# One adaLN-modulated transformer stack on one core: the first norm's modulation applied on transposed columns

## The reference, cut to what matters

```python
def rmsnorm(x, g):
    y = xf * lax.rsqrt(jnp.mean(xf * xf, axis=-1, keepdims=True) + EPS)
    return (y * g.astype(jnp.float32)).astype(x.dtype)

ada = (c @ w_ada + b_ada)[:, None, :]          # w_ada is (1024, 6144)
shift1, scale1, gate1, shift2, scale2, gate2 = jnp.split(ada, 6, axis=-1)
h = rmsnorm(x, g_norm1) * (1.0 + scale1) + shift1
proj = h @ w_in                                # q, k, v, gates, indexer: 12 parts
# fox attention (forget gates), indexer attention with a bias table,
# branches, w_out; rmsnorm + modulated MLP with squared relu; final rmsnorm
# then second_block: 2 layers, each swiglu FFN / mixer / swiglu FFN with layer norms
```

## Time and profile before

| | |
|---|---|
| median of three runs | 1501.1 us (1496.76 to 1505.11) |
| profiled execution | 1496.24 us |
| its span (first to last instruction) | 1494.5 us |
| mean granted TensorE clock | 0.977 |
| TensorE matmul busy | 1399.2 us, 94% |
| VectorE / ScalarE busy | 828.6 us, 55% / 644.4 us, 43% |
| GpSimd busy | 71.3 us, 5% |
| DMA | 268.87 MB, mean 180 GB/s |
| chain of waits, by engine | TensorE 80%, VectorE 8%, DMA 5%, ScalarE 3%, issue 3%, GpSimd 1% |

### The profile page before, as it was taken

How to read it: one execution, slowest core, us unless ns; L and a number is a source line. 1 busy time by engine, 2 the same in 40 slices (tenths; PEclk the granted TensorE clock), 3 DMA queues, 4 the chain that set the end, 5 groups by cost and what they waited for, 6 DMA issues and landing times.

```text
span 1494.5 us, 16234 instructions
## 1 busy us (share of the span) xinstructions
PE 1399.2 (94%) x6296; PEld 1123.1 (75%) x6296; DVE 828.6 (55%) x1117; ACT 644.4 (43%) x1029; POOL 71.3 (5%) x109
## 2 busy tenths in 40 slices
PE   2799999989999999999898999999999999899997
PEld 0577776768888778887776788887788877788886
DVE  6686642676665565455534665446555464755444
ACT  0454442534444354444455454334443344444332
POOL 3100000010000100000100100001000010100000
PEclk9999986999999999999999999999999999999999
DMA  8646753336645466454641565555755544575552
GB/s 309 213 166 199 230 160 100 142 115 223 254 171 198 129 213 207 181 182 157 215 151 59 175 193 206 185 162 167 243 175 181 185 151 160 194 226 172 187 179 84
DMA packets 156478, 268.87 MB, mean 180 GB/s; under 512 B 9543, under 2 KB 101735, under 8 KB 155250
## 3 DMA queue, kind: packets, MB, share of 16 engines
q1 hardware_dynamic: 148578, 239.43, 46.9%
q0 software_dynamic: 7824, 28.41, 5.9%
HBM read 266.74 MB, written 1.07 MB: 179 GB/s over the span
## 4 chain that ended last, share of the span: by engine, by line
PE 80%; DVE 8%; DMA 5%; ACT 3%; issue 3%; POOL 1%; SPq 0%; DVEq 0%; ACTq 0%; POOLq 0%
PE UP L579 15%; PE UP L581 15%; PE UP L580 15%; PE Y L579 8%; PE Y L580 8%; PE Y L581 8%; PE TB L631 3%; DVE WL L1234 3%; PE Y L657 1%; DMA RAW<-in_ffn_w_gu 1%; DMA RAW<-in_a_w_in 1%; ACT WH L948 1%; DMA X<-in_x 1%; DVE Z L1570 1%; PE Y L660 1%
## 5 line engine op out<-in xcount | busy, mean ns | idle before, releaser
L1234 DVE TENSOR_TENSOR WL<-RAW,WH 128x1024 fp32r<-128x1024 f32 (+2 forms) x448 | 510.2, 1193 | 234.2 <-ACT WH L948 231.1
L948 ACT CAST WH<-RAW 128x1024 fp32r<-128x1024 f32 (+2 forms) x448 | 430.4, 1031 | 263.3 <-PE Y L581 155.3
L579 PE MATMUL UP<-WH,AH 128*128 128x512 f32 (+1 forms) x1104 | 447.8, 406 | 22.8 <-issue 11.5
L581 PE MATMUL UP<-WH,AL 128*128 128x512 f32 (+1 forms) x1104 | 435.0, 394 | 0.0
L580 PE MATMUL UP<-WL,AH 128*128 128x512 f32 (+1 forms) x1104 | 434.3, 393 | 0.0
L579 PEld LDWEIGHTS UP<-WH,AH 128*128 128x128 f32 x1104 | 211.1, 191 | 68.0 <-issue 23.3
L581 PEld LDWEIGHTS UP<-WH,AL 128*128 128x128 f32 x1104 | 210.4, 191 | 45.0
L580 PEld LDWEIGHTS UP<-WL,AH 128*128 128x128 f32 x1104 | 211.5, 192 | 40.7 <-issue 0.7
L579 PE MATMUL Y<-WH,HH 128*128 128x512 f32 (+1 forms) x496 | 193.2, 390 | 0.0
L581 PE MATMUL Y<-WH,HL 128*128 128x512 f32 (+1 forms) x496 | 191.5, 386 | 0.0
L580 PE MATMUL Y<-WL,HH 128*128 128x512 f32 (+1 forms) x496 | 191.4, 386 | 0.0
(11 more groups left out here) (191 smaller groups left out, 965.9 us busy)
## 6 DMA issues: line engine op xcount, KB each, us to landing
RAW<-in_ffn_w_gu SPq DMA_DIRECT2D x176, 512.0 KB, 5.1
RAW<-in_ffn_w_down SPq DMA_DIRECT2D x80, 512.0 KB, 4.2
RAW<-in_w_mlp SPq DMA_DIRECT2D x64, 512.0 KB, 4.2
RAW<-in_w_in SPq DMA_DIRECT2D x40, 512.0 KB, 5.2
PIECE<-in_w_ada POOLq DMA_DIRECT2D x32, 512.0 KB, 4.2
RAW<-in_a_w_in SPq DMA_DIRECT2D x24, 512.0 KB, 4.7
WADA<-in_w_ada SPq DMA_DIRECT2D x8, 1024.0 KB, 10.5
RAW<-in_w_out SPq DMA_DIRECT2D x8, 512.0 KB, 3.9
```

The source lines that it names most:

```text
L579: pe.matmul(dst, ah, wh, start=first, stop=False)
L581: return pe.matmul(dst, al, wh, start=False, stop=last)
L948: act.copy(WH[:, u % 2, q * n:(q + 1) * n], RAW[:, q // 2, (q % 2) * n:(q % 2 + 1) * n]).then_inc(wh_done, 1)
L1234: ve.tensor_tensor(WL[:, u % 2, o], RAW[:, q // 2, (q % 2) * n:(q % 2 + 1) * n], WH[:, u % 2, o].bitcast(F32), ALU.subtract).then_inc(wl_d ...
```

## The change

The first norm's modulation is no longer applied on rows (tokens on partitions) but after the transposes, where a channel is a partition, so that scale and shift are one number per partition.

- c, b_ada's first 2048 and g_norm1 are loaded as 32 rows of 128 numbers, and one transpose makes them columns (COLS). The broadcast of g_norm1 and the one-partition load of b_ada go. w_ada's slab k now holds the rows k*128+p.
- ScalarE computes both tiles' sums of squares and x * rstd, copies the table row, and copies the transposed tiles to XT (laid over PIECE).
- VectorE runs the eight slabs in a row, the eighth in two halves of columns, each its own DMA.
- TensorE transposes both tiles, then for each half sums ADA with products of one moving column: ADA's 128x128 blocks are stationary, ONES[:, 0:1] moves.
- VectorE forms SCALE and SHIFT (128x4 per half) and MOD = XT * SCALE + SHIFT (laid over ROWS), ScalarE forms the rounded AH by the same operation, VectorE subtracts to AL. Each of the eight contraction blocks covers both tiles. This alternates with unit 0's weight quarters, and TensorE waits per block (mod_low).
- GpSimd reads the table back only behind the first two pieces; IDENT is built before its DMAs.

```diff
-            sp.dma_start(CC[:, :], t["c"][0].rearrange("(p k) -> p k", k=KT)).then_inc(in_c, 16)
-            sp.dma_start(PIECE[0:1, :, :], t["b_ada"][0:2 * D].rearrange("(o a n) -> o a n", o=1, a=2)
-                         ).then_inc(in_brow, 16)
-            wada = t["w_ada"].rearrange("(p k) n -> p k n", k=KT)
+            sp.dma_start(ROWCOL[24:32, :], t["c"][0].rearrange("(r p) -> r p", p=P)).then_inc(in_c, 16)
+            sp.dma_start(ROWCOL[0:16, :], t["b_ada"][0:2 * D].rearrange("(r p) -> r p", p=P)).then_inc(in_c, 16)
+            sp.dma_start(ROWCOL[16:24, :], t["g_norm1"].rearrange("(r p) -> r p", p=P)).then_inc(in_c, 16)
+            wada = t["w_ada"].rearrange("(k p) n -> p k n", p=P)
...
-            gp.dma_start(ROWS[:, 0, :], t["g_norm1"].partition_broadcast(P)).then_inc(in_rows, 16)
...
-            gp.wait_ge(tmp_v, TMP_V[("h", 1, 1)])
+            gp.wait_ge(ada_done, 2)
+            gp.wait_ge(mod_low, KT)
             step(gp.memset(ADA[:, :, :], 0.0))
...
-            pieces(0, PIECES + 2)
+            pieces(0, 2)
+            table_read(0)
+            pieces(2, PIECES + 2)
...
+            for tok in range(TOK):
+                pe.wait_ge(xhat_done, tok + 1)
+                chain_turns("h", tok, Z)
+            for h in range(2):
+                pe.wait_ge(*((acc_half, 1), (wada_used, KT))[h])
+                for a in range(2):
+                    for k in range(4 * h, 4 * h + 4):
+                        mm = pe.matmul(Y[0][h][:, 4 * a + k % 4:4 * a + k % 4 + 1], ADA[:, a, k * P:(k + 1) * P],
+                                       ONES[:, 0:1], start=True, stop=True)
+                mm.then_inc(ada_done, 1)
...
+            act.wait_ge(in_x, 16)
+            for tok in range(TOK):
+                for h in range(2):
+                    ins = act.activation(Z[:, tok, h * HALF:(h + 1) * HALF], X[:, tok, h * HALF:(h + 1) * HALF], ACT.Square,
+                                         scale=D ** -0.5, accum_out=SQ[:, tok, h:h + 1])
+                ins.then_inc(sq_done, 1)
+            taken(("tab", 0), REVROW[:, :], REV)
+            for tok in range(TOK):
+                act.wait_ge(rs_done, tok + 1)
+                act.activation(Z[:, tok, :], X[:, tok, :], ACT.Copy, scale=RS[:, tok:tok + 1]
+                               ).then_inc(xhat_done, 1)
+            for tok in range(TOK):
+                for h in range(2):
+                    taken(("h", tok, h), XT[:, 4 * h:4 * h + 4, tok * P:(tok + 1) * P], HALF)
+            def mod_highs(h):
+                act.wait_ge(scale_done, h + 1)
+                for k in range(4 * h, 4 * h + 4):
+                    act.activation(AH[:, k, :], XT[:, k, :], ACT.Identity, bias=SHIFT[:, k:k + 1],
+                                   scale=SCALE[:, k:k + 1]).then_inc(mod_high, 1)
             round_unit(0, (0, 1))
-            chain_high("h", 0)
+            mod_highs(0)
             round_unit(0, (2, 3))
+            mod_highs(1)
...
+            for h in range(2):
                 s = slice(h * HALF, (h + 1) * HALF)
+                k = KT - 1
+                ve.wait_ge(*((in_wada[k % 4], 32), (in_last, 16))[h])
+                ve.scalar_tensor_tensor(ADA[:, 0:2, s], WADA[:, k % 4, :].rearrange("p (a n) -> p a n", a=2)[:, :, s],
+                                        CC[:, k:k + 1], ADA[:, 0:2, s], ALU.mult, ALU.add
+                                        ).then_inc((acc_half, wada_used)[h], 1)
+            def modulated(h):
+                q = slice(4 * h, 4 * h + 4)
+                ve.wait_ge(ada_done, h + 1)
+                step(ve.tensor_tensor(SCALE[:, q], Y[0][h][:, 4:8], COLS[:, 8 + 4 * h:12 + 4 * h], ALU.add))
+                ve.tensor_tensor(SHIFT[:, q], Y[0][h][:, 0:4], COLS[:, q], ALU.add)
+                ve.tensor_tensor(SCALE[:, q], SCALE[:, q], COLS[:, 16 + 4 * h:20 + 4 * h], ALU.mult
+                                 ).then_inc(scale_done, 1)
+                ve.wait_ge(scale_done, h + 1)
+                for k in range(4 * h, 4 * h + 4):
+                    ve.tensor_scalar(MOD[:, k, :], XT[:, k, :], SCALE[:, k:k + 1], SHIFT[:, k:k + 1],
+                                     ALU.mult, ALU.add).then_inc(mod_done, 1)
+            def mod_lows(first, end):
+                for k in range(first, end):
+                    ve.wait_ge(mod_done, k + 1)
+                    ve.wait_ge(mod_high, k + 1)
+                    ve.tensor_tensor(AL[:, k, :], MOD[:, k, :], AH[:, k, :].bitcast(F32), ALU.subtract
+                                     ).then_inc(mod_low, 1)
+            split_unit(0, (0,))
+            for h in (1, 3):
+                ve.wait_ge(*emptied(TURN[("h", 1, h // 2)]))
+            modulated(0)
+            mod_lows(0, 2)
+            split_unit(0, (1,))
+            mod_lows(2, 4)
+            split_unit(0, (2,))
+            modulated(1)
+            mod_lows(4, 6)
+            split_unit(0, (3,))
+            mod_lows(6, 8)
```

More of the change, by code:

```diff
@@ L176 @@
 TMP_S = counts(lambda k: k[0] in BY_SCALAR)
-TMP_V = counts(lambda k: k[0] not in BY_SCALAR and k[0] not in ("tab", "flip", "ada", "F", "pool", "y", "my"))
+TMP_V = counts(lambda k: k[0] not in BY_SCALAR and k[0] not in ("col", "h", "tab", "flip", "ada", "F", "pool", "y", "my"))
 TG_NO = counts(lambda k: k[0] in ("up", "gu"))
@@ L476, in step @@
                 gp.wait_ge(g_seq, seq[0])
+            step(gp.memset(IDENT[:, :], 0.0))
+            step(gp.affine_select(out=IDENT[:, :], in_=IDENT[:, :], compare_op=ALU.not_equal, fill=1.0, base=0,
+                                  pattern=[[-1, P]], channel_multiplier=1))
             gp.dma_start(BF[:, :], t["b_forget"].partition_broadcast(P)).then_inc(in_small, 16)
@@ L484, in _ @@
             step(gp.memset(ONES[:, :], 1.0))
-            step(gp.memset(IDENT[:, :], 0.0))
-            step(gp.affine_select(out=IDENT[:, :], in_=IDENT[:, :], compare_op=ALU.not_equal, fill=1.0, base=0,
-                                  pattern=[[-1, P]], channel_multiplier=1))
             step(gp.affine_select(out=TRI[:, :], in_=ONES[:, :], compare_op=ALU.is_ge, fill=0.0, base=0,
@@ L593, in wide @@
                 for k in range(kts):
+                    if u == 0 and tok == 0:
+                        pe.wait_ge(mod_low, k + 1)
                     if chain and k % 4 == 0:
@@ L693, in slot @@
                     values(a - 1)
+            pe.wait_ge(g_seq, 2)
+            pe.wait_ge(in_c, 48)
+            pe.transpose(bank_of(("col",))[:, 0:32], ROWCOL[:, :], IDENT[0:32, 0:32]).then_inc(tr_done, 1)
             pe.wait_ge(in_small, 48)
@@ L717, in _ @@
             rev_row(0)
[L719 to L724, removed]
-            for row, h in parts:
-                pe.matmul(Y[row][h][:, :], ONES[:, :], ADA[:, row, h * HALF:(h + 1) * HALF],
-                          start=False, stop=True).then_inc(ada_done, 1)
-            chain_turns("h", 0, Z)
+            for tok in range(TOK):
[8 more added lines that the diff above has]
+                mm.then_inc(ada_done, 1)
             att = 0
@@ L1347, in _ @@
             ve.tensor_copy(IDR[:, :], IDENT[:, :]).then_inc(cmr_done, 1)
-            ve.wait_ge(in_c, 16)
+            ve.wait_ge(tr_done, TURN[("col",)] + 1)
+            ve.tensor_copy(COLS[:, :], TB[TURN[("col",)] % 2][:, 0:32]).then_inc(tr_free[TURN[("col",)] % 2], 1)
+            ve.wait_ge(*emptied(TURN[("col",)]))
+            step(ve.tensor_scalar(COLS[:, 8:16], COLS[:, 8:16], 1.0, None, ALU.add))
             acc = ADA[:, 0:2, :].rearrange("p a n -> p (a n)")
-            for k in range(KT):
+            for k in range(KT - 1):
                 ve.wait_ge(in_wada[k % 4], 16 * (k // 4 + 1))
@@ L1368, in _ @@
-            ve.wait_ge(in_rows, 16)
-            def modulated(tok, h):
-                s = slice(h * HALF, (h + 1) * HALF)
-                if tok == 0:
-                    ve.wait_ge(ada_done, 2 * h + 2)
-                    step(ve.scalar_tensor_tensor(ADA[:, 1, s], Y[1][h][:, :], 1.0, ROWS[:, 0, s], ALU.add, ALU.mult))
-                step(ve.tensor_tensor(Z[:, tok, s], Z[:, tok, s], ADA[:, 1, s], ALU.mult))
-                ve.tensor_tensor(Z[:, tok, s], Z[:, tok, s], Y[0][h][:, :], ALU.add).then_inc(tmp_v, 1)
@@ L1379, in _ @@
-            modulated(0, 0)
-            modulated(0, 1)
-            chain_low("h", 0)
-            split_unit(0)
-            modulated(1, 0)
-            modulated(1, 1)
-            chain_low("h", 1)
+            for h in range(2):
+                s = slice(h * HALF, (h + 1) * HALF)
+                k = KT - 1
[3 more added lines that the diff above has]
+                                        ).then_inc((acc_half, wada_used)[h], 1)
```

79 lines of the change are left out of this document (37 added, 42 removed).

## The result

The kernel after took 1490.18 us (median of eight runs, 1486.92 to 1495.57), the kernel before 1500.24 us in eight runs on the same chip (1496.53 to 1505.11). The ratio is 0.9933, with the interval [0.9912, 0.9954]: 6.9 to 13.2 us faster. The forecast was 1492 us in 1482 to 1500. The profiled execution took 1487.73 us with a span of 1484.6, at a mean granted clock of 0.977, as before; its span is 9.9 us shorter.

A forecast was written before the change was run, and what follows sets the result against it. The prediction took a chain of waits in the first 62 us as the bound; shorter slabs, modulation and splits let unit 1 start at 53.1 instead of 62.07, 9.0 us gained: median 1501.1 becomes 1492, range 1482 to 1500.

The forecast's parts named there:

- The bound: First 62 us: a chain of waits bounds the start; what is gained at 62.07 should arrive at the end.
- rival (c): Attention slots, 160 to 233 us: TensorE's clock shifts; three more slow periods lose 9.6 us; chance 0.07 slow, 0.08 lucky.
- The sum for the modulation: VectorE's w_ada slabs: with work moved to ScalarE they end at 31.9 instead of 35.5, 3.6 us gained.
- From the sum to the first matmul: One-column products and modulation ahead of unit 0: first matmul at 35.8 instead of 46.72, 10.9 us gained.
- Unit 0's split: VectorE's splits of unit 0's weights: the last WL ends at 41.4 instead of 48.86, 7.5 us gained.
- Unit 1's weights: DMA of unit 1's second half: 5.2 us from issue, landed 47.2 instead of 56.2, 9.0 us gained.
- Rival (b): Weight loads: unit 1's takes 6.91 us again, or table and pieces push unit 2's; gain 5.5, 1495.5 us; chance 0.13.
- Statistics: ScalarE's sums and GpSimd's roots: second root ready 27.6, copies done 31.2, before the products' end at 33.7.
- rival (a): GpSimd's roots come late behind VectorE's slab products, second at 30 to 32.4; gain 6.7, 1494 us; chance 0.12.
- hidden by 2.5 us: ScalarE's copies of the transposed tiles: done at 31.2, covered by the first half's products, which end at 33.7.
- At nothing: Costs taken as zero: the columns' transpose, copy and +1, table-row steps on ScalarE, the later table read.
- The number: Whole kernel: a median of 1492 us, against 1501.1 for the kernel before.

The follow-up runs named there:

- e5: The kernel after with the table's 1 MB read put back ahead of the modulation; 1490.69 us, ratio 0.9920.
- e8: The kernel after with the 512 KB broadcast of g_norm1 loaded again on GpSimd's queue; 1496.27 us, ratio 0.9970.
- e7: The kernel before with only the statistics, the scaled copy and the table row moved to ScalarE; 1496.49 us, ratio 0.9976.
- e1: The kernel after with all of unit 0 rounded and split before the modulation; 1485.40 us, ratio 0.9894.
- e10: The kernel after with 52 extra fp32 matmuls on constants ahead of TensorE's transposes; 1500.19 us, ratio 0.9999.
- e3: The kernel after with x loaded ahead of the first four slabs; 1490.15 us, ratio 0.9921.
- e4: The kernel after with the first half's eight one-column products issued twice; 1495.12 us, ratio 0.9971.
- e2: The kernel after with three small GpSimd loads and the table row moved behind the first half's sums; 1489.47 us, ratio 0.9919.

## Why the prediction was right, point by point

- **The bound.** Right in the main. What the change is shown to gain, it gains ahead of unit 1. "What is gained at 62.07 should arrive at the end" was too smooth: 1.6 us were lost up to the second norm, most of them by the clock at unit 1's start, and 3.6 came on top some 650 us later. The forecast named the attention slots of 170 to 240 us as the place where the clock may turn. Between the two kernels' profiles the number of long periods there didn't change (one of 12.95 us, at 200.80 to 213.75, and before one of 12.98, at 196.84 to 209.82, each with one of 11.4 behind it). But rival (c) is real: five of the variants' profiles have a further period of 13 us and are some 5 us longer there (e5). Whether the slower executions of the kernel after have it (clock down to 0.969) isn't shown.
- **The sum for the modulation**: 3.6 us gained by the slabs' end, 4.1 measured (31.45). e8 confirms the 1.3 us of the broadcast, with 1.4. The row order, the columns' loads and the 2 KB pieces cost little: e8 has them and e7 has not, both have the broadcast, and the slabs end 0.4 us apart (32.85 and 32.48).
- **From the sum to the first matmul**: the half's 16 instructions were priced at 3.0 us and took 3.29; the choice in the middle of 1.8 and 5.3 held. The four multiply-adds at 0.25 each took 1.15 on the path (0.29 each), the small steps 0.16. The first matmul came at 37.16 and not 35.8. That step failed: the second half's 16 instructions stand ahead of unit 0 in TensorE's order, and I had let unit 0 start between. It cost nothing, as unit 0 isn't on the path (e1).
- **Unit 0's split**: forecast 41.4, measured 41.92.
- **Unit 1's weights**: the term that was off most. I took 5.2 us from issue to landing, it was 6.02; with an issue 0.36 us later (42.36 for 42.0) the half lands 1.2 us late (48.38 for 47.2), and unit 1 starts 1.1 us late (54.24 for 53.1). The reason given, that half 0 just ahead in the queue had made it 6.91, isn't borne out either: in e1 the halves are issued 1.9 us apart and the load takes 5.77 us, in the kernel after they are 4.6 us apart and it takes 6.02, in e10, as far apart, 4.44. What sets this time is open. Rival (b) was half right: of its 1.7 us (6.91 for 5.2), 0.8 came.
- **Statistics**: the second root ends at 26.88, forecast 27.6, so rival (a) did not occur. Yet the "hidden by 2.5 us" was wrong, and this is the step of the mechanism that failed. The sum set the end of ScalarE's copies against the end of the products. But TensorE's order puts all transposes ahead of the products, and the second tile's transposes (28.67 in the chain) wait for ScalarE's first copy of the first tile, which ScalarE's order puts behind the second tile's scaled copy (to 28.05). From the root to the last transpose it took 3.7 us, to 30.6, where the first half's sum is there at 30.2. The cover was nothing, and it was luck that this cost no more than some tenths (e3). GpSimd's rows:

```profile
20.58 0.30 POOL L533 TENSOR_SCALAR VAR<-SQ 128x1 f32<-128x1 f32 x1 [14.38 <-ACT Z L1060]
20.96 0.57 POOL L534 TENSOR_TENSOR RS<-VAR,NHALF 128x1 f32<-128x1 f32 x1
21.78 2.34 POOL L533 TENSOR_SCALAR VAR<-SQ 128x1 f32<-128x1 f32 x1 [0.25 <-ACT Z L1060]
24.21 2.66 POOL L534 TENSOR_TENSOR RS<-VAR,NHALF 128x1 f32<-128x1 f32 x1
```

  The first tile's two instructions fell in the gap ahead of slab 4's product (0.30 and 0.57 us), the second's each lasted about until the slab product beside it was done. The Trainium skill, "SBUF — State Buffer", section "Who interferes with whom", says that a VectorE instruction with two SBUF inputs and a GpSimd one that reads SBUF contend for a port pair that is locked exclusively. By that rule the trace agrees, 2.34 and 2.66 us for work of 0.30 and 0.57.
- **At nothing**: the columns' transpose and its copy are done before slab 0's product, which now starts at 7.03; the table's move costs nothing at the start (e5).
- **The number.** 1492 was forecast against 1490.2. The agreement is closer than the parts: 1.2 us less at unit 1 and 1.6 less up to the second norm, 3.6 more from the late stretch, and the medians' own width of about 3 us. That these cancel is luck. The 7.8 us alone would be 0.52%.

## What to carry to other kernels

Ahead of a dense weight stream, ask what lets the next weights be issued, and do that first: here the split of the present unit, worth 4.8 us against 0.9 lost at its own start (e1). Move tiny loads out from under a large stream that the start waits for. And when a sum of columns is replaced by many one-column products, count each at TensorE's slow pace if it has been idle, and read from its hand-written order what stands ahead of them. Where the end of a long kernel moves by several us for reasons of its own, judge a change at the start by a mark close behind it.

## What the runs showed of the hardware

- An fp32 product with one moving column is two matmul instructions of 0.21 us each after an idle TensorE, 0.11 after a busy one (e4, e10).
- The granted clock in the profile can miss a slow stretch. In 38 to 42 us of the kernel after it reads 1.00, while the starts of unit 0's 332-column matmuls are 0.28 us apart; from 43.5 us on they are 0.15 apart. Before the change the same 0.28 stands in a stretch that reads 0.50 (the first row):

```profile
46.70:49.30 2.60, 2.58 (x9) 2.60 (x10) 2.60 (x4) 0.00 (x0) 0.00 (x0) 0.50 0.35 58
```

```profile
38.00:42.00 4.00, 3.95 (x15) 3.53 (x14) 3.93 (x12) 2.07 (x4) 0.00 (x0) 1.00 0.80 262
```

```profile
39.52 0.48 PE L599 MATMUL UP<-WH,AL 128*128 128x332 f32 x1
39.80 0.48 PE L597 MATMUL UP<-WH,AH 128*128 128x332 f32 x1
...
45.11 0.32 PE L599 MATMUL UP<-WH,AL 128*128 128x332 f32 x1
45.27 0.31 PE L597 MATMUL UP<-WH,AH 128*128 128x332 f32 x1
```

- 22 packets under 512 B held the 16 DMA engines for 90.2% of 1.5 us, about 1 us each, and without the three loads that they belong to the slabs end 2.1 us earlier (e2). The Trainium skill, "DMA: Bandwidth & Descriptors", section "Specifications", asks for at least 512 B for full rate; the trace agrees, with 68 GB/s moved in this stretch and 421 without them.
